# One rotated score term of MLA as two split products instead of one float32 product, in a hybrid decoder layer

## The reference, cut to what matters

```python
q = (rmsnorm(q_lat, q_norm) @ w_uq).reshape(B, S, 8, 128 + 64)
q_nope, q_rope = q[..., :128], q[..., 128:]
q_rope = rope(q_rope, cos[:, :, None], sin[:, :, None])     # 64 elements of each of 8 heads
k_rope = rope(k_rope, cos, sin)                             # one 64-element key, shared by all heads
s = einsum('bthd,bshd->bhts', qn, k_nope) + einsum('bthr,bsr->bhts', qr, k_rope)
p = masked_softmax(s * scale, kpos <= t)
# DSA: score[t, s] = sum over 8 index heads of iw * relu(iq . ik); the 128 best of a row are kept
```

## Time and profile before

| | |
|---|---|
| time, median of 3 runs | 1480.64 us (1480.25 to 1480.86) |
| profiled execution, its own time | 1480.7 us |
| its span in the trace | 1478.9 us |
| granted TensorE clock, mean | 0.999 of full |
| PE, DVE, ACT, POOL busy | 98%, 46%, 38%, 6% of the span |

### The profile page before, as it was taken

One profiled execution on the slowest core, in us unless ns is written; L12 is line 12 of the kernel. 1 busy time (PEld: TensorE's weight loads), 2 busy tenths in 40 slices (PEclk: granted clock), 3 DMA queues, 4 the chain that ended last, 5 costly groups with the idle time before them and its releaser, 6 DMA issues.

```text
span 1478.9 us, 17387 instructions
## 1 busy us (share of the span) xinstructions
PE 1455.6 (98%) x7212; PEld 1175.5 (79%) x7212; DVE 686.4 (46%) x1188; ACT 568.9 (38%) x920; POOL 94.3 (6%) x70
## 2 busy tenths in 40 slices
PE   7999999999999999999999999999999999999998
PEld 7867778887887788886776788887779888888886
DVE  5575757755233454465355244573354331223334
ACT  4455541224233334255345324453343432224221
POOL 0000000022120000000000110000000210012100
PEclk9999999999999999999999999999999999999999
DMA  7210223222221244540110424353121332232321
GB/s 209 61 45 31 72 86 109 91 86 79 92 81 62 66 142 145 169 129 20 53 57 30 156 86 142 95 180 106 48 86 58 114 101 99 89 111 86 109 91 57
DMA packets 118287, 137.87 MB, mean 93 GB/s; under 512 B 7060, under 2 KB 98449, under 8 KB 118209
## 3 DMA queue, kind: packets, MB, share of 16 engines
q1 hardware_dynamic: 115216, 126.17, 27.1%
q0 software_dynamic: 2704, 10.00, 2.0%
q10 hardware_dynamic: 288, 0.59, 0.1%
HBM read 134.61 MB, written 2.14 MB: 92 GB/s over the span
## 4 chain that ended last, share of the span: by engine, by line
PE 95%; DVE 2%; ACT 1%; issue 1%; DMA 1%; DVEq 0%; ACTq 0%
PE dense L676 26%; PE dense L678 26%; PE dense L677 25%; PE score L818 4%; PE turned L835 3%; PE score L835 3%; PE turned L818 2%; PE turned L828 1%; PE score L828 1%; DVE probs L1967 1%; PE score L1209 1%; DMA gain_row<-in_norm_gains 1%; ACT probsT L1311 0%; PE score L1195 0%; PE turned L1195 0%
## 5 line engine op out<-in xcount | busy, mean ns | idle before, releaser
L1801 DVE TENSOR_TENSOR weight_low<-raw,weight_high 128x2048 fp32r<-128x2048 f32 (+2 forms) x96 | 201.1, 2102 | 368.3 <-ACT weight_high L1311 368.2
L676 PE MATMUL dense<-hidden_high,weight_high 128*128 128x512 f32 (+1 forms) x840 | 326.7, 389 | 1.6 <-DVE hidden_low L2198 0.9
L678 PE MATMUL dense<-hidden_high,weight_low 128*128 128x512 f32 (+1 forms) x840 | 320.6, 382 | 0.0
L677 PE MATMUL dense<-hidden_low,weight_high 128*128 128x512 f32 (+1 forms) x840 | 320.2, 381 | 0.0
L1311 ACT ACTIVATE weight_high<-raw 128x2048 fp32r<-128x2048 f32 (+4 forms) x156 | 220.9, 1440 | 257.4 <-PE dense L678 253.6
L676 PEld LDWEIGHTS dense<-hidden_high,weight_high 128*128 128x128 f32 x840 | 158.0, 188 | 31.6 <-issue 1.5
L678 PEld LDWEIGHTS dense<-hidden_high,weight_low 128*128 128x128 f32 x840 | 157.9, 188 | 30.9
L677 PEld LDWEIGHTS dense<-hidden_low,weight_high 128*128 128x128 f32 x840 | 158.1, 188 | 29.6 <-issue 0.7
L1796 DVE TENSOR_TENSOR weight_low<-raw,weight_high 128x1024 fp32r<-128x1024 f32 x58 | 74.9, 1334 | 67.6 <-ACT weight_high L1311 67.6
L676 PE MATMUL dense<-weight_high,up_high 128*128 128x512 f32 x256 | 99.6, 389 | 0.0
L677 PE MATMUL dense<-weight_low,up_high 128*128 128x512 f32 x256 | 99.6, 389 | 0.0
(11 more groups left out here) (321 smaller groups left out, 2316.7 us busy)
## 6 DMA issues: line engine op xcount, KB each, us to landing
raw<-in_w_in SPq DMA_DIRECT2D x33, 1024.0 KB, 5.3
raw<-in_mlp_w SPq DMA_DIRECT2D x32, 1024.0 KB, 5.2
raw<-in_w_branch SPq DMA_DIRECT2D x12, 1024.0 KB, 5.1
raw<-in_nsa_cmp_w SPq DMA_DIRECT2D x8, 1024.0 KB, 5.4
raw<-in_cross_wkv SPq DMA_DIRECT2D x8, 1024.0 KB, 5.6
raw<-in_w_in SPq DMA_DIRECT2D x11, 512.0 KB, 5.3
bias_strips<-bias_scratch POOLq DMA_DIRECT2D x8, 512.0 KB, 4.3
raw<-in_w_out SPq DMA_DIRECT2D x4, 1024.0 KB, 5.0
```

The lines of the kernel that those rows point to most:

```text
L676: pe.matmul(out_ap, ah, bh, start=first, stop=False)
L677: pe.matmul(out_ap, ah, bl, start=False, stop=False)
L678: return pe.matmul(out_ap, al, bh, start=False, stop=last)
L1801: ins = V.tensor_tensor(dst, src, hi.bitcast(F32), ALU.subtract)
```

## The change

The rotated term of a score tile is no longer one float32 product on 128 partitions but two fp32r products. For head h the tile `qrS[h]` holds the high part of its 64 query elements on its own 64 partitions and the low part on the other 64; `krH` holds the high part of the key twice. So `qrS[h]` x `krH`, on 128 partitions, gives high x high + low x high. The third product, high x low, is on the 64 partitions of head h alone (`krL`).

- The weights' columns stay in the order of the heads, so the copies of a slab `uq` on ACT and DVE are two instead of three.
- `rotate` now works with halves of 32 partitions: six instructions instead of four. It ends in a semaphore `rope_turned`.
- GpSimd makes the split: two casts and two subtractions of 64x512 for each pair, then `rope_split`, for which PE waits instead of for DVE.
- `rotate_key` writes `krH` (2 casts) and `krL` (2 subtractions) instead of 4 copies; the two memsets are gone.
- `select(4 * p, 4)` stands ahead of `low(s + 3)` and `normalise`.

```diff
@@ PE, scores of a pair @@
-                pe.wait_ge(taken["V"], taken_count[product_at["m2", p]])
+                pe.wait_ge(rope_split, p + 1)
@@
+                        hi = slice(64 * h, 64 * h + 64)
                         score_tile((2 * p + h) * NT + i, [(qT[:, h, q], kT[:, h, 0:(i + 1) * P]),
-                                                          (qrT[:, q], krT[h][:, 0:(i + 1) * P])], (i + 1) * P)
+                                                          (qrS[h][:, q], krH[:, 0:(i + 1) * P]),
+                                                          (qrS[h][hi, q], krL[hi, 0:(i + 1) * P])], (i + 1) * P)
@@ DVE, rotate @@
                 V.tensor_tensor(dst[:, :], b[:, 0, :], cosT[:, :], ALU.mult)
-                V.tensor_tensor(ropeTmp[0:64, :], b[64:128, 0, :], sinT[64:128, :], ALU.mult)
-                link(V.tensor_tensor(ropeTmp[64:128, :], b[0:64, 0, :], sinT[0:64, :], ALU.mult))
-                V.tensor_tensor(dst[:, :], dst[:, :], ropeTmp[:, :], ALU.add).then_inc(taken["V"], 1)
+                for x in range(0, P, 64):
+                    V.tensor_tensor(ropeTmp[x:x + 32, :], b[x + 32:x + 64, 0, :], sinT[x + 32:x + 64, :], ALU.mult)
+                    ins = V.tensor_tensor(ropeTmp[x + 32:x + 64, :], b[x:x + 32, 0, :], sinT[x:x + 32, :], ALU.mult)
+                ins.then_inc(taken["V"], 1)
+                dve.wait_ge(taken["V"], taken_count[product_at[name]])
+                V.tensor_tensor(dst[:, :], dst[:, :], ropeTmp[:, :], ALU.add).then_inc(rope_turned, 1)
@@ DVE, rotate_key @@
-                dve.wait_ge(rope_zeroed, 2)
-                for h in range(2):
-                    for x in range(2):
-                        r = 64 * x + 32 * h
-                        V.tensor_copy(krT[h][r:r + 32, :], turns[32 * x:32 * x + 32, :])
+                V.tensor_copy(krH[0:64, :], turns[0:64, :]).then_inc(rope_key, 1)
+                V.tensor_copy(krH[64:128, :], turns[0:64, :])
...
+                dve.wait_ge(rope_key, 1)
+                for h in range(2):
+                    V.tensor_tensor(krL[64 * h:64 * h + 64, :], turns[0:64, :], krH[0:64, :].bitcast(F32), ALU.subtract)
@@ DVE, the loop over pairs @@
+                if p:
+                    dve.wait_ge(rope_split, p)
                 rotate(("m2", p), qrT)
@@
                 for h in range(2):
                     softmax_in((2 * p + h) * NT, h, lambda i, cols: strip0[:, T - cols:], MLA_SCALE)
+                select(4 * p, 4)
                 low(s + 3)
                 for h in range(2):
                     normalise(2 * p + h, h)
-                select(4 * p, 4)
@@ GpSimd @@
+            for p in range(4):
+                pool.wait_ge(rope_turned, p + 1)
+                for h in range(2):
+                    hi = slice(64 * h, 64 * h + 64)
+                    Q.tensor_copy(qrS[h][hi, :], qrT[hi, :]).then_inc(rope_high, 1)
+                for h in range(2):
+                    hi, lo = slice(64 * h, 64 * h + 64), slice(64 - 64 * h, P - 64 * h)
+                    pool.wait_ge(rope_high, 2 * p + h + 1)
+                    ins = Q.tensor_tensor(qrS[h][lo, :], qrT[hi, :], qrS[h][hi, :].bitcast(F32), ALU.subtract)
+                ins.then_inc(rope_split, 1)
```

More of the change, by code:

```diff
@@ L67, in shape_constants @@
     freq = np.float32(10000.0) ** (-(np.arange(0, ROPE, 2, dtype=np.float32)) / np.float32(ROPE))
-    turn = np.stack([freq[row % 32], np.where(row < 64, 1.0, -1.0)], 1).astype(np.float32)
+    turn = np.stack([freq[row % 32], np.where(row % 64 < 32, 1.0, -1.0)], 1).astype(np.float32)
     strip = np.zeros((P, T), np.float32)
@@ L114, in layer @@
         qrT = at("q_rope", [P, T], 190)
-        krT = [at("k_rope_even", [P, T], 192), at("k_rope_odd", [P, T], 124)]
+        qrS = [at("q_rope_stacked0", [P, T], 122, F32R), at("q_rope_stacked1", [P, T], 126, F32R)]
+        krH = at("k_rope_high_twice", [P, T], 192, F32R)
+        krL = at("k_rope_low_twice", [P, T], 124, F32R)
         cosT = at("cosT", [P, T], 194)
@@ L360, in split_pieces @@
                 d = wide(dst, 3, 384)[:, :, 0:256].rearrange("p k (h c) -> p k h c", h=2)
-                e = wide(dst, 3, 384)[:, :, 256:384].rearrange("p k (x h c) -> p k x h c", x=2, h=2)
+                e = wide(dst, 3, 384)[:, :, 256:384].rearrange("p k (h c) -> p k h c", h=2)
                 r = wide(src, 3, 384).rearrange("p k (h c) -> p k h c", c=192)
-                return [(d, r[:, :, :, 0:128]), (e[:, :, 0], r[:, :, :, 128:160]), (e[:, :, 1], r[:, :, :, 160:192])]
+                return [(d, r[:, :, :, 0:128]), (e, r[:, :, :, 128:192])]
             if slab_at["ukv", 0] <= s < slab_at["ukv", 0] + 8 and (s - slab_at["ukv", 0]) % 2 == 0:
@@ L519, in layer @@
         eps_ready = sem("eps_ready")
-        rope_zeroed = sem("rope_keys_zeroed")
+        rope_turned = sem("rope_turned")
+        rope_high = sem("rope_high_ready")
+        rope_split = sem("rope_split")
+        rope_key = sem("rope_key_high_ready")
         s_x = [sem(f"x_loaded{t}") for t in range(NT)]
@@ L1884, in rotate_key @@
                 V.tensor_tensor(turns[0:64, :], b[0:64, 0, :], cosT[0:64, :], ALU.mult)
-                V.scalar_tensor_tensor(ropeTmp[0:32, :], b[32:64, 0, :], -1.0, sinT[32:64, :], ALU.mult, ALU.mult)
+                V.tensor_tensor(ropeTmp[0:32, :], b[32:64, 0, :], sinT[32:64, :], ALU.mult)
                 link(V.tensor_tensor(ropeTmp[32:64, :], b[0:32, 0, :], sinT[0:32, :], ALU.mult))
                 link(V.tensor_tensor(turns[0:64, :], turns[0:64, :], ropeTmp[0:64, :], ALU.add))
-                dve.wait_ge(rope_zeroed, 2)
-                for h in range(2):
-                    for x in range(2):
-                        r = 64 * x + 32 * h
-                        V.tensor_copy(krT[h][r:r + 32, :], turns[32 * x:32 * x + 32, :])
+                V.tensor_copy(krH[0:64, :], turns[0:64, :]).then_inc(rope_key, 1)
+                V.tensor_copy(krH[64:128, :], turns[0:64, :])
                 V.tensor_copy(ikT[0:64, :], b[64:128, 0, :])
                 V.tensor_copy(ikT[64:128, :], b[64:128, 0, :]).then_inc(taken["V"], 1)
+                dve.wait_ge(rope_key, 1)
+                for h in range(2):
+                    V.tensor_tensor(krL[64 * h:64 * h + 64, :], turns[0:64, :], krH[0:64, :].bitcast(F32), ALU.subtract)
             low(slab_at["lat", 1] + 2)
@@ L2338, in _ @@
             Q = nc.gpsimd
-            Q.memset(krT[0][:, :], 0.0).then_inc(rope_zeroed, 1)
-            pool.wait_ge(x_scaled, NT)
-            Q.memset(krT[1][:, :], 0.0).then_inc(rope_zeroed, 1)
             pool.wait_ge(setup_taken, 1)
```

## The result

The changed kernel takes 1491.6 us (median; 1491.5 to 1492.8) against 1480.4 before (1480.2 to 1480.9): ratio 1.0077, 95% interval 1.0065 to 1.0089, 11.1 us slower. The forecast was 1493.5 (1486 to 1499). The profiled execution's span is 1489.7 us, 10.8 above the 1478.9 before. In the page's busy times PE is busy for 7.8 us more than in the earlier trace rows, with the same number of instructions; the other 3.0 us are idle time.

A forecast was written before the change was run, and what follows sets the result against it. The prediction took PE, busy 98% of the span, as the bound. From 1480.7 us it added 5.6 + 1.4 + 3.0 + 1.4 + 1.4 = 12.8, giving 1493.5 us, range 1486 to 1499.

The forecast's parts named there:

- Parts 1 to 3: Scoring: float32 term out (2.16 us a head), two fp32r products (0.63 each) and row changes (1.60) in; +5.6 us.
- A: Scoring: the change of row count costs nothing, an excursion of 0; 1480.7 us, not slower; chance 0.12.
- D: Row changes free in scoring, GpSimd's contention with DVE and PE's split waits cost nearly nothing; 1476.3 us; chance 0.06.
- B: Scoring: only the way back from 64 rows costs, 6.4 us less; 1487.1 us; chance 0.14.
- Part 4: Pair 0: two more rotation products on DVE make PE start the scores 1.4 us later.
- Part 5: Pair 0: GpSimd's split and DVE's index additions exclude each other, scores start 3.0 us later (bounds 0 and 4.3).
- One sign of the prediction: Ahead of the scores of pair 0, PE would wait for ACT's index tiles for 4 to 5 us.
- Parts 6 and 7: Pair 1: moved-up selection rounds delay the probabilities, +1.4 us; PE then waits for GpSimd's split, +0.7.
- Part 7: Ahead of the scores, PE waits for GpSimd's split: +0.7 us in pair 1, none in 2, +0.7 in 3.
- Rival C: GpSimd's unnamed instruction ahead of its first subtraction takes long; at 8 us PE waits 5 longer, 1498.5 us; chance 0.08.

The follow-up runs named there:

- Experiment 1: Changed kernel with the third product of a tile on all 128 partitions, so low x low is added too; 1479.7 us, ratio 0.9999 to the kernel before.
- experiment 4: Kernel before with only the longer rotation: four products of 32 rows instead of two of 64; 1484.1 us, ratio 1.0026.
- experiment 3: Changed kernel with GpSimd making four constant fills in pair 0 instead of the split, leaving out pair 0's rotated term; 1489.1 us, ratio 1.0062.
- experiment 6: Changed kernel with the selection rounds of pair 0 only back behind the normalisation; 1492.8 us, ratio 1.0083.
- experiment 2: Changed kernel with the 64-row products of two neighbouring tiles together, 16 excursions instead of 32; 1486.9 us, ratio 1.0048.
- experiment 7: Changed kernel with the selection rounds of all pairs back behind the normalisation; 1507.2 us, ratio 1.0181.
- experiment 8: Kernel of experiment 1 with DVE making the split, weight splits moved, and pair 0's rounds back behind the normalisation; 1479.5 us, ratio 0.9997.
- experiment 9: Kernel of experiment 8 with pair 0's split behind six of eight index additions, the last two behind normalising, PE waiting per head; 1479.8 us, ratio 0.9994.

## Why the prediction held, point by point

**Parts 1 to 3, +5.6: the mechanism right, the size 1.0 too large.** The head is 4.90 us by the trace, forecast 2.16 + 2.86 = 5.02. Experiment 1 splits it: without the row change the head takes 3.43, so 2.16 + 2 x 0.63 was right to 0.01; the excursion is 0.37 and not 0.40. By this head the four blocks cost 4 x 1.16 = 4.6. Within an excursion the load starts 0.19 after the columns of the matmul ahead, not 0.1, and its matmul starts at once; the sum of the two was right. Rivals A and D, with a free excursion, are out by experiment 1. B, with half the price, is out by the 0.37 and by the two loads at 143.74 and 144.18, which both wait. The Trainium skill, "TensorEngine Tiling (Array Packing)", section "Key Properties", says that changing the tiling mode drains TensorE; it gives no time for it. By that rule the trace agrees, with 0.37 us for a way in and out.

**Part 4, +1.4 in pair 0: measured 1.4** (experiment 4, counted from the start of the rotation). What the text said of the other pairs, that nothing is late there, holds only because the rounds moved; in the order of before the same rotation costs 2.5 more by the start of pair 3 (191.43 - 97.51 = 93.92 against 187.84 - 97.79 = 90.05, 3.9 in all).

**Part 5, +3.0: measured 2.2 to 2.3** (13.73 from the rotation to the scores, against 11.55 in experiment 3 and 11.45 in experiment 4). The step was right, that GpSimd's reads and DVE's instructions with two SBUF inputs exclude each other, and so was the price of GpSimd's four instructions. Their durations by the tile, in ns, shortest, median and longest, and the two casts of pair 3:

```profile
L2364 POOL CAST q_rope_stacked<-q_rope x8: 612/1050/2601, 102.0 to 194.1; 64x512 fp32r<-64x512 f32 x8
L2368 POOL TENSOR_TENSOR q_rope_stacked<-q_rope,q_rope_stacked x8: 1260/1267/1615, 104.2 to 196.1; 64x512 fp32r<-64x512 f32 x8
...
191.44 3.27 POOL L2364 CAST q_rope_stacked<-q_rope 64x512 fp32r<-64x512 f32 x2 [23.87 <-DVE q_rope L1888]
```

The shortest cast, 0.61 us, is the second of pair 3, the only one with no weight split of DVE beside it. The forecast had 0.6, which was a choice between 0 and 1.28 and hit by luck. The first cast of pair 3 takes 2.60 in the trace, because it begins 0.15 after DVE's weight split of 2.28 us; in the other pairs the two casts take 1.27 and 0.83, beside the two pieces of the split. A cast that takes longer has waited for DVE in it. A subtraction takes 1.26 where DVE leaves it alone, forecast 1.28.

What was too large is the share that falls on the start of the scores. Against experiment 4, which has the same rotation and no split, ACT's first relu starts 0.71 later, counted from the rotation (104.49 - 97.67 = 6.82 against 103.62 - 97.51 = 6.11), for DVE has the weight split beside the casts, and its first index instruction takes 0.83 instead of 0.48 beside the second one. The next relu starts 1.67 after the first instead of 0.86, another 0.81. From there to the last relu it is 4.24 (106.16 to 110.40) instead of 3.74, another 0.50, though the second slow addition takes 0.8 longer as well: in part it falls into time in which ACT had other work. That is 2.0 us. The fallen clock, which the prediction didn't have, comes on top: PE started the scores 0.74 after ACT's last relu in experiment 4 (108.22 to 108.96) and 1.00 after it here (110.40 to 111.40), so it has 0.3.

One sign of the prediction did not come as it was written: PE waits for ACT's index tiles for 2.1 us in all and not for 4 to 5. The start is still 3.7 late, because the 13 dense products ahead of it run at the low clock, by 0.21 instead of 0.12 us each, 1.2 us in which PE is busy and would otherwise have waited.

The trace now has a row for the kind of DVE instruction that the earlier trace rows couldn't show, one that reads PSUM and a single SBUF tensor. Timeline of DVE in pair 1, during GpSimd's subtractions from 136.63:

```profile
136.54 0.69 DVE L2000 TENSOR_TENSOR branch_out_low<-score,branch_out_high 128x512 fp32r<-128x512 f32 x1 [0.46 <-ACT branch_out_high L1318]
```

It takes 0.69 us, as before the change. The Trainium skill, "SBUF — State Buffer", section "Who interferes with whom", says so of an instruction with at most one SBUF input outside the 2-port modes; by that rule the trace agrees.

**Parts 6 and 7 in pair 1, +1.4 and +0.7: together 2.0 us.** From the end of the scores of pair 0 to the start of those of pair 1 it was 16.0 us and is 18.0. Of this 1.22 is the wait for the probabilities and 0.25 that for the split; the remaining 0.5 has no row of its own. The sum is right, but the two are not independent terms (experiment 6).

**Part 7 in pairs 2 and 3, 0 and +0.7: measured 0 and 0.49.** The form was right: only where the weight split is one piece is GpSimd kept waiting long (both casts together 3.27 at 191.44 in place of 2.16). The split is ready 18.5 us after the end of the scores of the pair before in pair 2 and 19.6 in pair 3 (197.38 - 177.78), both as forecast. The 0.2 too much come from the other side: the sum took pair 2's 18.9 for when PE wants to start in pair 3, where the kernel before had 187.84 - (160.12 + 8.64) = 19.1.

**Rival C, the unnamed instruction on GpSimd: out.** The casts start at 101.96 and take 2.15, and the subtractions start at 104.20, 0.09 later.

Between the two profiles the sum is 3.6 + 2.0 + 0.1 + 0.5 for the starts and 4 x 1.16 for the blocks, 10.8; forecast were 4.4 + 2.1 + 0 + 0.7 and 5.6, 12.8. Each delay came in its place and with its cause. Half of the 2.0 too much is the price of the excursion, most of the rest Part 5; the clock, with its 0.3, hides a little of that.

## What to carry to other kernels

A matmul on 64 rows between matmuls on all 128 wasn't cheaper here but dearer, by 0.37 us each: fill the other rows with zeros or a useful term (only the useful term was run), or put such products together. Where an engine that is 47% busy sits in a chain with the bound one, the order in its queue decides each added instruction: take the waits one after the other, look for what stands in the queue in front of the instruction that is waited for, and put it where the engine idles. An edit that loses alone (the moved rounds) can be what another edit needs, so test both alone and together. And before a delay is read from two traces, count from a common instruction ahead of it: here that turned 1.1 us into 1.4.

## What the runs showed of the hardware

The change of the row count costs 0.37 us for the way in and out, and 0.40 where two 64-row products share it (experiments 1 and 2).

GpSimd and DVE take turns by whole instructions when GpSimd reads SBUF and DVE reads two SBUF tensors: a cast of 0.61 us took 2.60 when it began 0.15 after a DVE subtraction of 2.28, which kept its 2.28, and two DVE additions of 0.83 took 1.67 each from start to start beside GpSimd's subtractions. With fills instead of reads (experiment 3) the additions kept their 0.83. The index instruction ahead of them, which reads one SBUF tensor, took 0.83 beside a cast and 0.65 beside the fills, and 0.48 in the kernel before.

TensorE's granted clock fell from its upper level (2.4 GHz) to 1.2 GHz behind short waits, in a kernel in which PE is 98% busy. In the changed kernel PE had waited 1.57 and 0.54 us at the index products, and soon after that the 256-column matmuls follow every 0.21 us instead of every 0.12, timeline of PE:

```profile
108.08 0.28 PE L682 MATMUL dense<-weight_low,latent_high 128*128 128x256 f32 x1
108.20 0.29 PE L683 MATMUL dense<-weight_high,latent_low 128*128 128x256 f32 x1
...
110.12 0.41 PE L681 MATMUL dense<-weight_high,latent_high 128*128 128x256 f32 x1
110.33 0.41 PE L682 MATMUL dense<-weight_low,latent_high 128*128 128x256 f32 x1
```

It fell there in all five profiled kernels with these index products and the split beside them: from 108 to 112 the granted clock is 0.57 in the changed kernel, 0.61 in experiment 2, and 0.50 in experiments 1, 6 and 7. In experiment 3, with waits of 0.97 and 0.36 there, and in the kernel before, with none but the 0.36, it did not fall. In the profiled execution of experiment 8 it did not fall after 1.91 either, and in that of experiment 9 not after 2.03, though other executions of the same two kernels have a lower mean clock. What decides it is left open. It cost 0.3 us ahead of the scores in the changed kernel, some 1.3 more in the profiled executions of experiments 1 and 6, and most in experiment 7, where it also followed waits of 3 and 4 us.
